# Retention's output product taken out of the retention loop, as seven half-size products; the recurrence's output product dealt out over all 32 retention steps

## The reference, cut to what matters

```python
h = rms_norm(x, in_norm_g)
q, k, v, g, xr, gr, m_ret, m_rnn = split(h @ w_in)      # 1024 x 10240
q = rotary(q); k = rotary(k) / 16                       # 4 heads of 256
o = head_norm(retention(q, k, v))                       # 4 heads of 512, chunks of 128 tokens
y_ret = (silu(g) * o) @ w_ret_o                         # 2048 x 1024   <- changed
xr = causal_depthwise_conv(xr); hr = rg_lru(xr)         # 4 blocks of 256
y_rnn = (hr * gelu(gr)) @ w_rnn_o                       # 1024 x 1024   <- moved
mixed = sigmoid(m_ret) * y_ret + sigmoid(m_rnn) * y_rnn
x = x + mixed @ w_out
x = x + (silu(gate) * val) @ w_down                     # conv-gated MLP behind another norm
out = rms_norm(x, final_norm_g)
```

## Time and profile before

| | before |
|---|---|
| time, median of 3 | 2014.41 us (2014.01 to 2016.21) |
| the profiled execution's own time | 2014.26 us |
| its span, first to last instruction | 2012.5 us |
| TensorE busy | 1983.8 us (99%), 9304 matmuls |
| VectorE (DVE) busy | 1380.0 us (69%) |
| ScalarE (ACT) busy | 908.7 us (45%) |
| GpSimd (POOL) busy | 232.8 us (12%), 188 instructions |
| mean granted TensorE clock | 0.998 of full speed |
| DMA | 285.10 MB, mean 142 GB/s |

### The profile page before, as it was taken

The page is one execution under the profiler, slowest core; times in us unless marked ns, Lnnn a source line. Parts: engine busy times, 40 slices in busy tenths (PEclk is TensorE's granted clock), DMA queues, the critical chain, the costliest instruction groups (busy, mean ns, idle before and its releaser), DMA issues.

```text
span 2012.5 us, 25123 instructions
## 1 busy us (share of the span) xinstructions
PE 1983.8 (99%) x9304; PEld 1656.6 (82%) x9304; DVE 1380.0 (69%) x1661; ACT 908.7 (45%) x1155; POOL 232.8 (12%) x188
## 2 busy tenths in 40 slices
PE   8999999999999999999999999999999999999998
PEld 7788888888888888887888888898788888888887
DVE  6977776776644444614876776747988788776766
ACT  6443344344445555412544543245644545543335
POOL 0000000010000000001255554300000000000000
PEclk9999999999999999999999999999999999999999
DMA  6343454444544343445334234731222122156533
GB/s 256 116 167 112 160 182 152 167 174 159 188 168 167 146 157 126 146 152 188 110 119 125 76 123 146 259 127 63 91 82 99 66 80 104 63 183 232 204 101 132
DMA packets 185636, 285.10 MB, mean 142 GB/s; under 512 B 9824, under 2 KB 123872, under 8 KB 185312
## 3 DMA queue, kind: packets, MB, share of 16 engines
q1 hardware_dynamic: 165264, 206.62, 30.9%
q0 software_dynamic: 20304, 77.60, 9.9%
HBM read 200.29 MB, written 83.89 MB: 141 GB/s over the span
## 4 chain that ended last, share of the span: by engine, by line
PE 83%; DVE 9%; ACT 3%; issue 2%; DMA 1%; POOL 1%; SPq 1%; DVEq 0%; POOLq 0%; ACTq 0%
PE ps L329 27%; PE ps L331 27%; PE ps L330 27%; POOL msg L888 1%; DVE ws L312 1%; DVE wx L2009 1%; PE ps L1130 1%; DMA raw<-w_rnn_o 0%; DMA qkv<-scr_v 0%; DVE sc L2055 0%; ACT ri L1530 0%; DVE th L2195 0%; DVE th L2199 0%; DVE ri L2206 0%; DVE gel L2209 0%
## 5 line engine op out<-in xcount | busy, mean ns | idle before, releaser
L1384 ACT ACTIVATE wx<-raw 128x1024 fp32r<-128x1024 f32 (+1 forms) x152 | 137.4, 906 | 253.0 <-DVE raw L1985 132.5
L329 PE MATMUL ps<-xs,wx 128*128 128x512 f32 x612 | 239.0, 390 | 2.1 <-DVE xs L2431 1.6
L331 PE MATMUL ps<-xs,wx 128*128 128x512 f32 x612 | 238.2, 389 | 0.0
L330 PE MATMUL ps<-xs,wx 128*128 128x512 f32 x612 | 238.1, 389 | 0.0
L2009 DVE TENSOR_TENSOR wx<-raw,wx 128x1024 fp32r<-128x1024 f32 (+1 forms) x152 | 156.3, 1029 | 31.5 <-ACT wx L1384 31.4
L329 PE MATMUL ps<-sc,wx 128*128 128x512 f32 x448 | 174.4, 389 | 3.0 <-ACT ub L1419 3.0
L331 PE MATMUL ps<-sc,wx 128*128 128x512 f32 x448 | 174.3, 389 | 0.0
L330 PE MATMUL ps<-sc,wx 128*128 128x512 f32 x448 | 174.3, 389 | 0.0
L329 PEld LDWEIGHTS ps<-xs,wx 128*128 128x128 f32 x612 | 114.9, 188 | 28.4 <-issue 2.7
L1419 ACT ACTIVATE ub<-ps 128x512 f32<-128x512 f32 x112 | 66.7, 597 | 156.8 <-PE ps L331 154.2
L331 PEld LDWEIGHTS ps<-xs,wx 128*128 128x128 f32 x612 | 114.9, 188 | 24.0
(11 more groups left out here) (282 smaller groups left out, 4808.9 us busy)
## 6 DMA issues: line engine op xcount, KB each, us to landing
raw<-w_in SPq DMA_DIRECT2D x80, 512.0 KB, 5.4
scr<-ost POOLq DMA_DIRECT2D x32, 1024.0 KB, 5.3
raw<-w_up SPq DMA_DIRECT2D x44, 512.0 KB, 3.9
tq<-w_down SPq DMA_DIRECT2D x88, 128.0 KB, 3.0
scr_t<-tq POOLq DMA_DIRECT2D x22, 512.0 KB, 3.2
scr_h<-vt POOLq DMA_DIRECT2D x11, 1024.0 KB, 4.3
scr_v<-ost POOLq DMA_DIRECT2D x8, 1024.0 KB, 4.6
qkv<-scr SPq DMA_DIRECT2D x64, 128.0 KB, 3.1
```

Source lines behind the costliest of these rows:

```text
L329: pe.matmul(out, w(HI), x(HI), start=first, stop=False, skip_group_check=True)
L330: pe.matmul(out, w(HI), x(LO), start=False, stop=False, skip_group_check=True)
L331: return pe.matmul(out, w(LO), x(HI), start=False, stop=last, skip_group_check=True)
L1384: act.activation(dst, src, ACT.Copy).then_inc(sem["f_hi"], 1)
```

## The change: what it does

- `w_ret_o`'s product becomes a stage of its own behind retention: y_ret's 1024 x 1024 result with 2048 inner rows is cut into halves on all three sides and made as seven products of half-size operands. It runs in 28 chunks of 24 matmuls (`reto(i, tiles)`), each with its own 512 KB weight load, and splits on ACT and DVE. The gated outputs go to DRAM (`scr_yg`) in each retention step by a new DMA on SP (`y_store`) and are loaded back as quarters (`yq`).
- The four sums of weight quarters this needs (t1 to t4) are made during the input projection's last four blocks, by POOL: 16 pieces, for each 4 loads, 3 additions or subtractions and a store to `scr_q`, all issued by POOL. Their buffer `tr` (three deep) lies in the A21 space.
- The load of A21 goes behind the last store of these pieces.
- `y_rnn`'s product is cut into 128 units of 3 matmuls, 4 in each of the 32 retention steps, 2 ahead of `update` and 2 behind it. Its weight splits come at step 4 of heads 0 to 2. The first chunk's loads wait until TensorE has done six of the eight half-block jobs of `LAST_PAIR`. Retention's loop is written out; the first head's special cases (buffers, low parts on DVE) are gone.
- The order of loads ahead of the `w_out` product changes: both weight blocks, then half of x, then the merge operands 8 to 11.

The core of the diff:

```diff
@@ POOL, input projection
+            def reto_pieces(j):
+                k, cols, v = j // 2, j % 2 * BC, j % 3
+                if j >= 3:
+                    pool.wait_ge(sem[f"tr_out{v}"], 16 * (j // 3))
+                for slot, r, n in ((0, 1, 1), (1, 0, 1), (2, 0, 0), (3, 1, 0)):
+                    row, col = (r * R_KT + k) * P, n * HALF + cols
+                    pool.dma_start(tr[:, v, slot, :], w_to[row:row + P, col:col + BC]).then_inc(sem[f"tr_in{v}"], 16)
+
+            def reto_combine(j):
+                k, cols, v = j // 2, j % 2 * BC, j % 3
+                pool.wait_ge(sem[f"tr_in{v}"], 64 * (j // 3 + 1))
+                pool.tensor_tensor(tr[:, v, 0:2, :], tr[:, v, 0:2, :], tr[:, v, 1:3, :], ALU.subtract).then_inc(late_sem("tr_st"), 1)
+                pool.wait_ge(*late_count("tr_st", 3 * j + 1))
+                pool.tensor_tensor(tr[:, v, 2, :], tr[:, v, 0, :], tr[:, v, 2, :], ALU.add).then_inc(late_sem("tr_st"), 1)
+                pool.wait_ge(*late_count("tr_st", 3 * j + 2))
+                pool.tensor_tensor(tr[:, v, 3, :], tr[:, v, 3, :], tr[:, v, 2, :], ALU.subtract).then_inc(late_sem("tr_st"), 1)
+                pool.wait_ge(*late_count("tr_st", 3 * j + 3))
+                pool.dma_start(scr_q[:, k * P:(k + 1) * P, cols:cols + BC].rearrange("q p c -> p q c"), tr[:, v, :, :]
+                               ).then_inc(sem[f"tr_out{v}"], 16)
+
             for b in range(IN_BLOCKS):
                 if b in W_AT:
                     store_tq(W_AT.index(b))
+                if b == LAST_QK + 2:
+                    pool.wait_ge(sem["rot_done"], 16)
+                    reto_pieces(0)
+                    reto_pieces(1)
+                if b >= LAST_QK + 2:
+                    for j in range(4 * (b - LAST_QK - 2), 4 * (b - LAST_QK - 1)):
+                        if j + 2 < R_PIECES:
+                            reto_pieces(j + 2)
+                        reto_combine(j)
                 store(*in_pair(b), rows(IN_COL[b]))
@@ SP, A21's load back: from ahead of block 28's load to behind round 0's loads
-                if b == IN_BLOCKS:
-                    sp_.wait_ge(sem["rot_done"], 16)
-                    sp_.wait_ge(sem["tq_out"], 16 * W_TILES)
+                if n == 0:
+                    sp_.wait_ge(sem["tq_out"], 16 * W_TILES)
+                    for v in range(3):
+                        sp_.wait_ge(sem[f"tr_out{v}"], 16 * len(range(v, R_PIECES, 3)))
                     sp_.dma_start(actv[:, 1, 0, :, :, :].bitcast(F32).rearrange("p a k c -> p (a k c)"), scr_a
                                   ).then_inc(sem["a21_in"], 16)
@@ SP, retention
-            for slot in range(2):
-                sp_.wait_ge(blk[slot], PAIR_RNNO + 1)
-            chunk_load(0, 0)
+            sg_load(0)
+            load_columns(sp_, *rnno_pair(1), w_ro, BC)
+            chunk_load(0)
...
+                chunk_load(r)
+                gate_load(r - 1)
+                if r >= 3:
+                    y_store(r - 3)
@@ SP, ahead of w_out
+            for m in range(2):
+                sp_.wait_ge(*late_count("rw_lo", R_CHUNKS - 1 + m))
+                load_columns(sp_, *out_block(m), w_o, m * BC)
+            sp_.wait_ge(*late_count("ry_lo", R_CHUNKS - 4))
+            sp_.dma_start(x1[:, 0:4, :], x_t[:, 0:4, :]).then_inc(sem["x_re"], 16)
+            for n in range(8, 12):
+                mix_load(n)
@@ TensorE, retention
-                scores(h, j)
-                turn_out(*previous(h, j, 2))
-                outs(*previous(h, j))
-                update(h, j)
-                for n in reto_parts(h, j):
-                    reto(*n)
+            for r in range(32):
+                scores(r)
+                if r >= 2:
+                    turn_out(r - 2)
+                if r:
+                    outs(r - 1)
+                for unit in range(4 * r, 4 * r + 2):
+                    rnno_unit(unit)
+                if r % 8 < 7:
+                    update(r)
+                for unit in range(4 * r + 2, 4 * r + 4):
+                    rnno_unit(unit)
+            turn_out(30)
+            outs(31)
...
+            reto(0, (0, 1, 3))
+            turn_out(31)
+            reto(0, (2,))
+            for i in range(1, R_CHUNKS - 1):
+                reto(i, (0, 1, 3, 2))
+            reto(R_CHUNKS - 1, (0, 1, 2, 3))
@@ ScalarE, retention step
                 if j < 7:
                     act.wait_ge(sem["t_done"], h * 7 + j + 1)
+                    act.activation(state_s[:, slot, HI, :, :], state[:, :, :], ACT.Copy).then_inc(sem["s_hi"], 1)
+                if j == 4 and h < 3:
+                    split_hi(act, *rnno_pair(h + 1))
@@ VectorE, behind the 28 chunks
+            mixed(8)
+            mixed(9)
+            split_lo(dve, *out_block(0))
```

More of the change, by code:

```diff
@@ L686, in _, with mix_load @@
+            stored_y(14)
+            reto_y(1, 0, 1, 0, "y22a")
+            reto_y(1, 0, 1, 4, "y22b")
+            gate_load(31)
+            y_store(29)
+            reto_w(2)
+            y_store(30)
+            sp_.wait_ge(blk[1], PAIR_RNNO + 3)
+            reto_y(2, 0, 0, 0, "y21a")
+            reto_y(2, 0, 0, 4, "y21b")
+            reto_w(3)
+            y_store(31)
             w_o = a["w_out"][0]
-            for n in range(16):
-                half, t = n // 8, n % 8
+            def mix_load(n):
+                half, t = mix_at(n)
@@ L1620, in step @@
-                if (j == 3 and not first) or j == 5:
-                    split_hi(act, h + PAIR_RETO, 0 if j == 3 else 1)
-                if j < 7:
-                    act.wait_ge(sem["t_done"], h * 7 + (j + 1))
-                    act.activation(sts_of(h, j)[:, slot, HI, :, :], stt_of(h, j)[:, :, :], ACT.Copy).then_inc(sem["s_hi"], 1)
-                if first and j == 1:
-                    split_hi(act, PAIR_RETO, 0)
-            for j in range(2):
-                qk_hi(0, j)
-                v_hi(0, j)
@@ L1631, in _ @@
[L1631 to L1648 removed]
+                act.activation(scs[:, slot, HI, :], sc[:, slot, :], ACT.Copy).then_inc(sem["sc_hi"], 1)
@@ L2347, in step @@
                     else:
-                        last = dve.tensor_copy(stt[:, :, :], ps[:, 3:5, :])
+                        last = dve.tensor_copy(state[:, :, :], ps[:, 3:5, :])
                     last.then_inc(sem["t_done"], 1)
-                for n in parts[:1]:
-                    accumulate(*n)
-                if (j == 3 and not first) or j == 5:
-                    split_lo(dve, h + PAIR_RETO, 0 if j == 3 else 1)
-                if first and j == 2:
-                    split_lo(dve, PAIR_RETO, 0)
@@ new lines, in reto_add @@
+            def reto_add(p, half, n):
+                dve.wait_ge(*late_count("r_b", 4 * p + 4))
+                dve.wait_ge(*late_count("r_cp", 8))
+                cols = slice(half * HALF, (half + 1) * HALF)
+                for q in range(2):
+                    t, bank = slice(4 * n + 2 * q, 4 * n + 2 * q + 2), D_BANK[p] + 2 * q
+                    dve.tensor_tensor(yacc[:, t, cols], yacc[:, t, cols], ps[:, bank:bank + 2, :], ALU.add
+                                      ).then_inc(sem["acc"], 1)
@@ L2406, in _ @@
+            mixed_lo(11)
+            for n in range(13, 16):
                 mixed(n)
```

807 lines of the change are left out of this document (423 added, 384 removed).

## The result

The changed kernel takes 2119.35 us (median of 4 runs, 2117.05 to 2122.28), the kernel before 2014.21 us beside it. The ratio is 1.0518 (95% interval 1.0505 to 1.0531): slower by 105 us. I forecast 2075 us, 2046 to 2102. The direction was right and the time 44 us too small, outside the range.

A forecast was written before the change was run, and what follows sets the result against it. The prediction took TensorE's work as the bound (busy 1983.8 of 2012.5 us). It summed 2014.3 - 21.7 + 64 + 7 - 3.5 + 3 + 8 + 4 = 2075 us, range 2046 to 2102.

The forecast's parts named there:

- Matmuls removed, 21.7 us: y_ret's product: 768 matmuls become 672; the 96 removed, at 0.226 us spacing each, gain 21.7 us.
- POOL's loop, 64 us: End of input projection: POOL's 16 weight-sum pieces delay A21's reload to 692.1 us, so TensorE stands some 64 us late.
- the rival with 80 us: POOL's chain is dearer (additions held by DVE, dearer loads, later landings): 80 us, 2091 us in all; chance 0.15.
- The lock between DVE and POOL: Weight sums: POOL's additions could wait for DVE's two-input instructions, ending the loop some 8 us later, mostly already paid.
- Weight split at step 4, 7 us: Retention, step 4 of three heads: the split delays the transposed k for `update`, 2.3 us three times, +7 us.
- Transposed k, -3.5 us: Retention: two units now ahead of `update` cover the old waits for the transposed k, -3.5 us.
- Start of retention, 3 us: First chunk: its loads have 10.9 us of cover against 12 plus SP's 1 MB loads; 3 us net charged.
- Chunk loads in retention: Retention: SP's new `y_store` carries no charge; if its cover goes, chunk loads come late, up to 1 us a step.
- Ahead of w_out, 8 us: Between last chunk and w_out: DVE's first weight split queues behind merges 8 and 9, behind 4 MB of loads; 8 us.
- Clock, 4 us: Three new TensorE stops (A21, first chunk, w_out) each cost at least 1.4 us at the lower clock: 4 us.
- POOL's cheap end: Weight-sum loop with its cheap terms and a faster A21 load: TensorE 47 us late.
- the first rival: POOL's chain holds, but retention, first chunk and `w_out` run without new stops: 2055 us; chance 0.25.

The follow-up runs named there:

- the last run: Changed kernel with all repairs together, then DVE's sums re-placed and w_out's third weight block moved ahead of the merges: 2004.45 us, ratio 0.9942 to the kernel before.
- the run without sums: Changed kernel without POOL's weight-sum loads, additions and stores, chunks reading plain quarters of w_ret_o, A21 loaded back where it was before: 2045.69 us, ratio 1.0158.
- the swapped run: Changed kernel with two statements exchanged: POOL adds up and stores piece j before issuing the loads of piece j + 2: 2082.44 us, ratio 1.0333.
- the run with 256 KB gates: Changed kernel with the recurrence gates' 1 MB load in heads 1 to 3 split into four 256 KB loads, one every two steps: 2108.55 us, ratio 1.0465.
- the other repairs: Changed kernel with sums on DVE, w_out splits first, 256 KB gates, halved weight splits, earlier chunk loads and later second yq load: 2023.01 us, ratio 1.0037.
- one long stop: Kernel before, with A21 loaded back at the later place six times in a row, each after the last landed: 2045.36 us, ratio 1.0153.
- halves: Changed kernel with the weight split of heads 1 to 3 halved, ACT's in steps 3 and 4, DVE's in 5 and 6: 2109.81 us, ratio 1.0474.

## Why the prediction was right or wrong

- **Matmuls removed, 21.7 us.** Right, but visible only in the last run, where TensorE no longer stops.
- **POOL's loop, 64 us.** The mechanism was right in every part, the term too small: 75.3 us. The loads were too dear in my sum (44.8 us; measured 34.3, under their cheap end), the rest too cheap: additions with their gaps 48.0, measured 57.0, their dear end; the 13 turns from a store's issue to the next loads 41.6, measured 53.1, above their dear end of 51. Nine of these turns took 3.5 us, with an issue of `ost` inside or without one, as I had it; four took 4.9 to 6.8. The reload took 11.2 us and not 10.5. The range of this term, 47 to 88, held it, and the rival with 80 us was nearer than my 64. That the four stops come from this loop is shown by the run without sums; that only its end counts, by POOL's own rows, which wait for nothing but its pieces. Of the 75.3 us, 69.1 are TensorE standing still and 6.2 slower work, that behind the first three stops; the sum below counts the first as stops and the second as clock.
- **The lock between DVE and POOL.** I gave it some 8 us by the rule and had mostly paid it. What the 256-element additions took above their medians of 0.73 us is 16 x 0.22 + 16 x 0.10 = 5 us. One such pair, POOL's and DVE's in order of time:

```profile
588.96 1.59 POOL L902 TENSOR_TENSOR tr<-tr 128x256 f32<-128x256 f32 x1
```
```profile
588.40 1.56 DVE L2116 TENSOR_TENSOR wx<-raw,wx 128x1024 fp32r<-128x1024 f32 x1
```

  POOL's addition ends 0.6 us after DVE's subtraction does. The Trainium skill (SBUF — State Buffer, "SBUF: two separate sides") says that the later of the two waits for the whole instruction of the other; the trace agrees, here with 0.9 us. In the swapped run it was 16 x 0.41 + 16 x 0.07 = 8 us.
- **Weight split at step 4, 7 us.** Right to the tenth: three waits of 2.4 us.
- **Transposed k, -3.5 us.** Right: none but those three is left.
- **Start of retention, 3 us.** Nearly: waits of 4.0 and 0.7 us.
- **Chunk loads in retention.** The step that failed by its mechanism. I wrote that SP's new DMA has no charge and that "if that cover goes, chunk loads come late". I weighed `y_store`, but not the 1 MB loads in the same queue: 13.8 us of waits in four steps. In three steps, 10.7 us, it is the moved recurrence's load, and the run with 256 KB gates took 10.8 us back, clock included. In step 31, 3.1 us, it is most likely the new stage's first `yq` load; that was changed only together with the other repairs, where the wait is gone.
- **Ahead of w_out, 8 us.** The chain was named rightly and mis-sized: 14.0 us, inside its ends of 2 and 16.
- **Clock, 4 us.** The term that failed by most: 21.6 us. I counted three stops and took 1.4 us for each, "at least". Both were low, the number above all. By the clock records TensorE was at half clock in twelve stretches ahead of the last 20 us, before in one, and was busy for 4.0 us on average in each, so 2.0 us are lost (1.4 to 3.1). By differences between runs a stop costs 1.1 to 1.7 us (one long stop, halves, 256 KB gates), which is rougher.

The sum again with measured terms, on the profiled execution's span of 2012.5: -21.7 + 21.6 (clock) + 69.2 (four stops) + 17.8 and 0.7 (chunks) + 7.2 - 3.5 (k) + 14.0 (w_out) + 3.4 (retention product's operands) = 108.7, against 104.9 measured; the remaining 4 us are small waits that the kernel before had and this one has not, which I did not take apart. Of my miss of 44 us, the clock is 17.6, the unforeseen chunk waits 13.8, `w_out` 6.0, the loop's stops 5.2, the product's operands 3.4, the start 1.7 and the weight split 0.2, together 47.9, less those 4 us. No single term would have saved the forecast. The ends of my range don't follow from their own terms either: POOL's cheap end with the first rival is 2014.3 - 21.7 + 47 - 3.5 + 2 = 2038 and not 2046, the dear end 2075 + 24 = 2099 and not 2102. And its top held nothing for the number of stops or for a wait that I had not seen.

## What to carry to other kernels

When a change puts many small steps on one engine's queue, write the loop as one period (issues, work, landing) and multiply; then look at the order of two statements before the hardware: here one exchange was worth 37 of 75 us. Where TensorE is the bound, count the stops, not only their length: here each of 3.1 us and more, and some of 2.4, was followed by half clock once. A stop ahead of a new stage is seldom one instruction: what waits behind the first block stands behind the second too, so a repair is judged by where the stop goes. And weigh each transfer that a moved stage brings along, above all large ones in the queue that feeds the steps.

## What was not expected of the hardware

- POOL issues a 128 KB load in 0.54 us, where its 1 MB and 512 KB stores take 0.71 and 0.78.
- The same 512 KB store landed in 3.2 to 6.5 us with a median of 3.2, and leaving out the additions made the landings slower (3.3 to 9.0, median 4.2) and the waits for them longer, not shorter (40.0 to 50.9 us).
- After a stop of 3.6 us TensorE was busy at half clock about as long (6 us) as after 22 or 28.5 us (5 and 4 us), and after stops of 3.0 us at 78.8 and 2.4 us at 982.4 not at all.
- An issue on SP's queue grew from 0.5 to 2.3 us while 1 MB transfers were under way.
